# Dealing the turns of a two-layer decoder kernel anew: gate slices unit by unit, x loaded in smaller first parts from ScalarE's queue, narrower warm-up products

## Reference

```python
proj = h @ w_in                       # NSA: 1024 x 3632; HGRN2: 1024 x 4096
# layer 0 (NSA): q | k,v compressed | k,v selected | k,v window | gates | z
p_c = masked_softmax(q @ k_cmp, m_c)  # compressed branch; also picks the selected blocks
p_s = masked_softmax(q @ k_sel, m_s)
p_w = masked_softmax(q @ k_win, m_w)
o = g0 * (p_c @ v_cmp) + g1 * (p_s @ v_sel) + g2 * (p_w @ v_win)
x = x + (o * silu(z)) @ w_out
# layer 1 (HGRN2), per head: f, k = 1 - f, q, v from proj
state = exp(b_last) * state + (k * exp(b_last - b)).T @ v
o = (q * exp(b)) @ state + causal(q k^T * decay) @ v
x = x + (rmsnorm(o) * g_norm * silu(z)) @ w_out
out = rms_norm(x, final_norm)
```

## Time and profile before

| | us |
|---|---|
| median of 3 runs (318.56 to 318.68) | 318.58 |
| profiled execution | 319.03 |
| its span, first to last instruction | 316.8 |
| TensorE busy in the span | 307.6 |
| VectorE busy | 240.4 |
| ScalarE busy | 183.8 |

### The profile page before, as it was taken

One profiled execution on the slowest core, in us unless ns is written; L12 is line 12 of the kernel. 1 busy time (PEld: TensorE's weight loads), 2 busy tenths in 40 slices (PEclk: granted clock), 3 DMA queues, 4 the chain that ended last, 5 costly groups with the idle time before them and its releaser, 6 DMA issues.

```text
span 316.8 us, 5853 instructions
## 1 busy us (share of the span) xinstructions
PE 307.6 (97%) x2228; PEld 262.8 (83%) x2228; DVE 240.4 (76%) x423; ACT 183.8 (58%) x387; POOL 47.0 (15%) x51
## 2 busy tenths in 40 slices
PE   7999999999999999999999999999999989999993
PEld 5899788878899788877788889999997768888882
DVE  3969987899799878988748824477878997498941
ACT  4885262467794775866545744775264307897432
POOL 1003003031412341656000100000000100222000
PEclk9999999999999999999999999999999999999998
DMA  7999894756604800160270984374915233002011
GB/s 226 398 383 356 275 371 149 240 228 139 128 2 92 177 0 2 24 241 2 72 263 6 357 290 155 115 260 134 336 69 173 94 129 142 1 2 66 2 66 66
DMA packets 27819, 49.34 MB, mean 156 GB/s; under 512 B 2376, under 2 KB 6736, under 8 KB 27792
## 3 DMA queue, kind: packets, MB, share of 16 engines
q1 hardware_dynamic: 24896, 44.32, 43.0%
q10 hardware_dynamic: 2384, 2.63, 2.5%
q0 software_dynamic: 512, 2.03, 1.9%
HBM read 47.92 MB, written 1.05 MB: 155 GB/s over the span
## 4 chain that ended last, share of the span: by engine, by line
PE 78%; DVE 15%; issue 3%; DMA 2%; ACT 1%; SPq 0%; DVEq 0%; ACTq 0%
PE bank L589 73%; DVE w_lo L1105 3%; PE bank L768 2%; DVE nmax L1353 2%; DMA x_res<-in_x 2%; DVE qk L1164 1%; DVE prob_t L1365 1%; PE bank L633 1%; PE bank L691 1%; ACT prob L974 1%; DVE y_hg L1433 1%; DVE zT L1309 1%; PE bank L835 1%; DVE y_hg L1427 0%; DVE q L1280 0%
## 5 line engine op out<-in xcount | busy, mean ns | idle before, releaser
L1105 DVE TENSOR_TENSOR w_lo<-raw,w_hi 128x1024 fp32r<-128x1024 f32 (+1 forms) x80 | 86.8, 1138 | 19.3 <-ACT w_hi L865 19.3
L865 ACT ACTIVATE w_hi<-raw 128x1024 fp32r<-128x1024 f32 (+1 forms) x80 | 72.6, 966 | 15.7 <-PE bank L589 12.4
L589 PE MATMUL bank<-w_hi,h_hi 128*128 128x512 f32 x192 | 78.0, 406 | 0.0
L589 PE MATMUL bank<-w_hi,h_lo 128*128 128x512 f32 x192 | 75.1, 391 | 0.0
L589 PE MATMUL bank<-w_lo,h_hi 128*128 128x512 f32 x192 | 74.9, 390 | 0.0
L589 PE MATMUL bank<-h_hi,w_hi 128*128 128x256 f32 x224 | 64.7, 289 | 0.0
L589 PE MATMUL bank<-h_hi,w_lo 128*128 128x256 f32 x224 | 63.4, 283 | 0.0
L589 PE MATMUL bank<-h_lo,w_hi 128*128 128x256 f32 x224 | 63.4, 283 | 0.0
L589 PEld LDWEIGHTS bank<-h_lo,w_hi 128*128 128x128 f32 x224 | 42.9, 192 | 0.3
L589 PEld LDWEIGHTS bank<-h_hi,w_hi 128*128 128x128 f32 x224 | 43.0, 192 | 0.2
L589 PEld LDWEIGHTS bank<-h_hi,w_lo 128*128 128x128 f32 x224 | 42.9, 192 | 0.0
(11 more groups left out here) (207 smaller groups left out, 400.4 us busy)
## 6 DMA issues: line engine op xcount, KB each, us to landing
raw<-in_hg SPq DMA_DIRECT2D x16, 1024.0 KB, 7.0
raw<-in_nsa SPq DMA_DIRECT2D x10, 1024.0 KB, 7.6
raw<-in_nsa_out SPq DMA_DIRECT2D x8, 512.0 KB, 8.3
raw<-in_hg_out SPq DMA_DIRECT2D x4, 1024.0 KB, 6.2
raw<-in_nsa SPq DMA_DIRECT2D x2, 1120.0 KB, 7.4
raw<-in_nsa SPq DMA_DIRECT2D x8, 256.0 KB, 5.8
w<-in_w1k SPq DMA_DIRECT2D x2, 1024.0 KB, 12.8
w<-in_w1v ACTq DMA_DIRECT2D x2, 1024.0 KB, 6.8
```

Source lines behind the costliest of these rows:

```text
L589: return nc.tensor.matmul(o, lhsT, rhs, start=start, stop=stop, skip_group_check=True)
L865: m = nc.scalar.activation(dst, src, ACT.Copy)
L1105: m = V.tensor_tensor(lo, src, hi.bitcast(F32), ALU.subtract)
```

## The change

- `x` is loaded in three parts of each 128-row block (256, 256 and 512 columns). SyncE issues the first part of block 0 and the two wide parts; ScalarE issues the other three small ones before its table load. The bytes are the same.
- `HEAD` takes the first weight piece before the first pieces of `x`.
- The warm-up products are 2 of 256 columns, then 1 and 3 of 128, in place of 2, 1 and 2 of 256.
- `Z_ORDER` takes both token blocks of `V_Z0`, then both of `V_Z1`; before, the units alternated.
- `ORDER`, `H_ORDER`, `SPREAD`, `LAG`, `Z_LAG`, `CMP_LAG` and `PROD_LAG` have new values. The instructions and their shapes are otherwise the same.

```diff
-IDLE = (2, 1, 2)
+IDLE = ((S, 2), (P, 1), (P, 3))
-Z_LAG = 3
-Z_ORDER = [(V_Z0, 0), (V_Z1, 0), (V_Z0, 1), (V_Z1, 1)]
+Z_LAG = 2
+Z_ORDER = [(V_Z0, 0), (V_Z0, 1), (V_Z1, 0), (V_Z1, 1)]
-PROD_LAG = (5, 2)
+PROD_LAG = (4, 2)
-H_ORDER = 'aaaahhbbbbcccchhddeeeeddfFfFFFffFFFQFQQQQQQQGGGRGGGGGRRRRRRRzzllllzzllllzzllllzllllzllllzllllzzllllzoozxxzzzyyoommmyymnnnrrnrsrsss'
+H_ORDER = 'aaaahhbbbbcccchhddeeeeddfFfFFFffFFFQFQQQQQQQGGGGGRGGGRRRRRRzRzzllllzzzllllzzllllllllzllllzlllzzlzllllozoxxzzyyoommmyymnnnnsrrrrsss'
-FIRST_LOADS = [("x", 0, 0), ("w", 0), ("w", 1), ("x", 1, 0), ("w", 2), ("w", 3), ("x", 0, 1), ("x", 1, 1),
-               ("w", 4), ("w", 5), ("w", 6), ("w", 7)]
+X_PARTS = [slice(0, 2 * P), slice(2 * P, 4 * P), slice(4 * P, D)]
+FIRST_LOADS = (('x', 0, 0), ('w', 0), ('w', 1), ('w', 2), ('x', 0, 2), ('w', 3), ('x', 1, 2), ('w', 4), ('w', 5), ('w', 6), ('w', 7))
+ACT_LOADS = ((1, 0), (0, 1), (1, 1))
-CMP_LAG = 3
+CMP_LAG = 6
+        def load_x(eng, t, part):
+
+            cols = X_PARTS[part]
+            eng.dma_start(x[:, t, cols], t_in["x"][t * P:(t + 1) * P, cols]).then_inc(x_in[t][part], 16)
...
-                    for _ in range(IDLE[step[1]]):
-                        mm(bank[0][:, 0:S], rp[:, 0, 0:P], rp[:, 0, 0:S], True, True)
+                    wide, times = IDLE[step[1]]
+                    for _ in range(times):
+                        mm(bank[0][:, 0:wide], rp[:, 0, 0:P], rp[:, 0, 0:wide], True, True)
...
-                        pe.wait_ge(x_in[t][q // 2], 16)
+                        pe.wait_ge(x_in[t][min(q, 2)], 16)
...
+            for t, part in ACT_LOADS:
+                load_x(act, t, part)
```

More of the change, by code:

```diff
@@ L77 @@
 PROD_W = HD + HD // 2
-PROD_LAG = (5, 2)
+PROD_LAG = (4, 2)
 RECT_LV = (LAST_LV - 2, LAST_LV - 1)
-ORDER = 'HHAAHBHHBAAAHAHBBBABABCDCCrBCDDDgxEEFkGkEgFEFKIFIgIKKpIKgxLpkppgJkgqqgqsqszzszatgzztssbszztzszszzzctssvvvvtstsztzzavtsztvvvtststbsstvvvvtssostotsosctsvvvvttsvvttottvvvvtovvooo'
+ORDER = 'HHHAABHHHBAABAAHBABABBCDCCrCBDDDgxgEkEFGEEIKFFkFKIIKqIggKxppLkpkpgJgqqgszqsszzgatzzbsszzttzzszztcszsstvvvvstztzsavtsszztvvvtstsstsstbvvvvtssottosovvtcsvvtststvvtottvvvvtovvooo'
 HT_BANKS = ((4, 5, 6, 7), (0, 1, 4, 5))
-H_ORDER = 'aaaahhbbbbcccchhddeeeeddfFfFFFffFFFQFQQQQQQQGGGRGGGGGRRRRRRRzzllllzzllllzzllllzllllzllllzllllzzllllzoozxxzzzyyoommmyymnnnrrnrsrsss'
+H_ORDER = 'aaaahhbbbbcccchhddeeeeddfFfFFFffFFFQFQQQQQQQGGGGGRGGGRRRRRRzRzzllllzzzllllzzllllllllzllllzlllzzlzllllozoxxzzyyoommmyymnnnnsrrrrsss'
 CMP_BANKS = ((1, 1, 7), (7, 6, 1))
@@ L207, in split_places @@
     return places
-HEAD = [part for q in range(4) for t in range(TT)
-        for part in (("w", 2 * q + t), ("h", t, 2 * q), ("h", t, 2 * q + 1))]
-HEAD[0:4] = HEAD[1:3] + HEAD[0:1] + HEAD[3:4]
-FIRST_LOADS = [("x", 0, 0), ("w", 0), ("w", 1), ("x", 1, 0), ("w", 2), ("w", 3), ("x", 0, 1), ("x", 1, 1),
-               ("w", 4), ("w", 5), ("w", 6), ("w", 7)]
+HEAD = (('w', 0), ('h', 0, 0), ('h', 0, 1), ('w', 1), ('h', 1, 0), ('h', 1, 1), ('w', 2), ('h', 0, 2), ('h', 1, 2), ('h', 0, 3), ('h', 1, 3), ('w', 3), ('w', 4), ('h', 0, 4), ('h', 0, 5), ('w', 5), ('h', 0, 6), ('h', 0, 7), ('w', 6), ('w', 7), ('h', 1, 4), ('h', 1, 5), ('h', 1, 6), ('h', 1, 7))
+X_PARTS = [slice(0, 2 * P), slice(2 * P, 4 * P), slice(4 * P, D)]
+FIRST_LOADS = (('x', 0, 0), ('w', 0), ('w', 1), ('w', 2), ('x', 0, 2), ('w', 3), ('x', 1, 2), ('w', 4), ('w', 5), ('w', 6), ('w', 7))
+ACT_LOADS = ((1, 0), (0, 1), (1, 1))
 H_RANK = {part[1:]: n + 1 for n, part in enumerate(part for part in HEAD if part[0] == "h")}
@@ L222, in split_count @@
     return kk + 1 if u == 0 else KT + NQ * (u - 1) + kk // 2 + 1
-SPREAD = {U_KW: (0, 0, 3, 2), U_Q0: (7, 6, 29, 0), U_Q1: (0, 59, 13, 61), U_Z0: (0, 0, 4, 2), U_Z1: (3, 8, 5, 0), U_O0: (22, 18, 7, 37), U_O1: (44, 82, 83, 135), V_V0: (0, 2, 2, 2), V_V1: (0, 0, 26, 21), V_F0: (0, 0, 41, 5), V_Q0: (11, 3, 19, 73), V_F1: (0, 0, 6, 2), V_Q1: (3, 2, 26, 12), V_Z0: (1, 6, 2, 0), V_Z1: (2, 0, 14, 49), V_O0: (1, 3, 2, 5), V_O1: (5, 0, 2, 3)}
+SPREAD = {U_KW: (0, 0, 28, 27), U_Q0: (0, 20, 60, 2), U_Q1: (15, 41, 21, 43), U_Z0: (0, 3, 0, 0), U_Z1: (1, 8, 0, 9), U_O0: (11, 0, 8, 39), U_O1: (43, 103, 105, 152), V_V0: (0, 2, 0, 1), V_V1: (2, 0, 32, 42), V_F0: (0, 0, 23, 0), V_Q0: (11, 11, 12, 99), V_F1: (2, 3, 1, 2), V_Q1: (3, 2, 25, 9), V_Z0: (2, 3, 11, 22), V_Z1: (7, 0, 3, 55), V_O0: (9, 9, 0, 6), V_O1: (4, 0, 0, 1)}
 GATED_LAG = 6
-CMP_LAG = 3
+CMP_LAG = 6
 GATED_AT = [max(LAST[("pv", job)], LAST[Z_GROUPS[-1]] + job) for job in range(4)]
-LAG = {U_O0: 1, U_O1: 5, V_Z0: 4, U_Z0: 1, U_Q1: 10, V_O1: 2, V_Q0: 8, V_F1: 3, V_Z1: 4, V_F0: 8, V_V1: 2, U_Z1: 4, U_KW: 2, U_Q0: 2, V_V0: 1, V_O0: 2, V_Q1: 4}
+LAG = {U_O0: 11, U_O1: 6, V_Z0: 13, U_Z0: 3, U_Q1: 14, V_O1: 1, V_Q0: 1, V_F1: 4, V_Z1: 2, V_F0: 1, V_V1: 1, U_Z1: 3, U_KW: 2, U_Q0: 5, V_V0: 3, V_O0: 4, V_Q1: 1}
 SPLIT_HI_AT, SPLIT_LO_AT = split_places()
@@ L343, in program @@
         w1_in = [sem(f"w1_in{kv}") for kv in range(2)]
-        x_in = [[sem(f"x{t}_in{half}") for half in range(2)] for t in range(TT)]
+        x_in = [[sem(f"x{t}_in{part}") for part in range(len(X_PARTS))] for t in range(TT)]
         const_in = sem("const_in")
@@ L565, in _ @@
                         if what[0] == "x":
-                            _, t, part = what
-                            half = slice(part * UW, (part + 1) * UW)
-                            sp.dma_start(x[:, t, half], t_in["x"][t * P:(t + 1) * P, half]).then_inc(x_in[t][part], 16)
+                            load_x(sp, *what[1:])
                         else:
```

## The result

The changed kernel takes 321.25 us in the median of five runs (320.22 to 323.13; a sixth, disturbed one took 777.61, is left out of all comparisons, and would make the median 321.51) against 318.61 before: slower, ratio 1.008 with an interval of 1.0062 to 1.0098. 316.2 had been forecast, with a range up to 317.9. The profiled execution takes 321.78, its span is 319.7.

What follows compares the result with a forecast made beforehand. TensorE's queue of products was taken as the bound, busy 307.6 of 316.8 us. Head -0.2, changes of kind -1.0, attention -0.6 and levels -0.6 gave -2.4: 316.6 profiled, 316.2 for the median, range 315.3 to 317.9.

Steps and rivals of the forecast that it cites:

- rival (d): Head: the shorter warm-up lets TensorE's 1.2 GHz level last beyond 7.28; 317.6 (chance 0.04) or 319.6 (0.08).
- the slow end: Head: products run at half speed from 7.3 to about 14.5; +3.4, 319.6 us, chance 0.08.
- the milder case of (d): Head: the first three slices run at half speed, 0.6 hidden in the wait for x; +1.4, 317.6, chance 0.04.
- Head: Start of the kernel: transposes that waited for x until 9.9 come earlier; -0.2, between -0.5 and +0.1.
- 1,024 KB, again 7.24: Head: small x parts and two weight pieces total 1,024 KB, so they land at 7.24 as before.
- Fewer changes of kind: TensorE's order: 100 switch groups between fp32r products and other work in place of 112, ten at 0.1; -1.0.
- Rival (a): TensorE's order: switches cost nothing that can be had back; -1.4 in all, 317.2, chance 0.12.
- Attention: Attention: the prob_t copy comes 1.0 earlier on VectorE, so TensorE's waits of 0.52 and 0.2 shrink; -0.6.
- what is late next is the copy behind it, by 0.1 or 0.2: Attention: once the 0.52 wait is gone, the following copy is late by only 0.1 or 0.2.
- rival (b): Attention and levels: waits only move along VectorE's queue; -1.2, 317.4, chance 0.13.
- Levels: Recurrence levels: TensorE's two waits for decays shrink from 1.34 to about 0.7; -0.6, ends -1.3 and +0.3.

Runs made afterwards that it cites:

- e1: The changed kernel with the old loads, HEAD, warm-up products and first 19 letters of ORDER: 319.40 us, ratio 1.0026 to the kernel before.
- e5: The kernel before with the new head, but warm-up products all 256 columns wide as before: 319.32 us, ratio 1.0018.
- e2: The kernel before with the new head alone (two-queue loads, HEAD, narrow warm-up products, first 19 letters of ORDER): 320.94 us, ratio 1.0074.
- e7: The kernel before with the new head and narrow warm-up products, but all parts of x issued by SyncE: 319.18 us, ratio 1.0018.
- e11: The kernel before with the new head, all x parts issued by SyncE and warm-up products 256 wide: 319.01 us, ratio 1.0013.
- e10: The kernel before with two levels of the recurrence each cut in two by a gate slice (H_ORDER): 319.10 us, ratio 1.0015.
- e4: The kernel before with the new tables of layer 0 alone, without the new head: 319.88 us, ratio 1.0036.
- e3: The kernel before with the new tables of layer 1 alone (H_ORDER, Z_ORDER, PROD_LAG, V_ entries of SPREAD and LAG): 318.44 us, ratio 0.9991.
- e6: The kernel before with only the new, shorter warm-up products (2 of 256, then 1 and 3 of 128 columns): 319.56 us, ratio 1.0026.
- e15: The kernel before with the new tables of layer 0 alone, but CMP_LAG 5 in place of 6: 321.00 us, ratio 1.0073.

## Why the prediction was wrong

**The sign** fell twice: with the head (+2.2) and with the tables of layer 0 (+1.1). Either would have been enough against the 0.3 that layer 1 gained; e1, with the old head, is at ratio 1.0026. The larger part of the head's loss is rival (d), the clock: with wide warm-up products it is 0.5 (e5), with the new ones 2.2 (e2). The mechanism was named, on the evidence of the earlier trace rows, and given 0.12 in all and 0.08 for the slow end. Two steps made it too small. It was priced as if only the level at the start could last longer; in fact a raised array also falls back (8.7 to 12.07 in the profile after). And I put the landing of the last small part at 7.24 and reckoned only with the shorter warm-up: the late `x` made the idle time 1.16 and 0.67 us. The price of the clock itself was about right for the milder case of (d), three slices at half speed for +1.4: the eight products from 8.72 to 12.07 take 3.35 us, where at 0.23 each they take 1.84, a loss of 1.5. The slow end of (d) reckoned with twice that stretch; that the change ended on its side is due to layer 0 and to the changes of kind, not to the clock.

**Head, -0.2 predicted, +2.2 measured (e2).** The step that failed first is "1,024 KB, again 7.24". I named the other order, in which the third weight piece stands ahead of the last small part, and gave it 7.9 and +0.1; it landed at 8.2. The loads ran slower as well: in the changed kernel 185 and 212 GB/s were moved in the third and fourth microsecond, against 283 and 330 before. With the same small parts on one queue it was 204 and 319 (e7): the slow fourth microsecond goes with the two queues; why the third is slow isn't shown. What the forecast said of the far side was right: earlier products would only wait for the wide part of block 1 (e7, e11). With a sound warm-up and one queue the head is worth +0.2, not -0.2.

**Fewer changes of kind, -1.0 predicted, about 0 by the times of turns (no run has it alone).** Rival (a) was right for the groups that the change removes. I read half of a row pair: the second product of a slice starts late, but the turns ahead of it end early by the same amount. The groups that cost something, 0.35 each, are those of level products (e10), and the change has seven of them, as before: it joins two levels and cuts another in two. The count was generous too: taking slices against everything else, the strings have 87 changes before and 81 now, not 112 and 100.

**Attention, -0.6 predicted, +1.1 measured in e4 and 1.2 in its timeline, for all tables of layer 0.** The two waits for `prob_t` went, as forecast. But "what is late next is the copy behind it, by 0.1 or 0.2" was wrong: 0.5 at the normalized scores of block 0, 0.2 for GpSimd's `prob`, and small delays at other turns. By the shortest turns of the same kind and neighbours, the excess of TensorE's turns in layer 0 is 1.0 before and 2.1 in e4, of which the list of waits shows 0.7 in each. This goes the way of rival (b), but (b) had the gain come to nothing, and here it turned into a loss. Which entry of the tables makes it stays open: no single one that I tried brings it back, and the old places of the splits don't fit the new order.

**Levels, -0.6 predicted, -0.3 measured (e3).** The mechanism was right and its place too: two waits, at the second of the two levels that follow each other. They are 0.56 and 0.41, as in this timeline of the changed kernel:

```profile
262.70 1.12 PE L591 MATMUL bank<-qk 128*64 128x32 f32 x32 [0.56 <-DVE qk L1169]
264.23 1.13 PE L591 MATMUL bank<-qk 128*64 128x32 f32 x32 [0.41 <-DVE qk L1169]
```

The term was mis-sized: I had 0.4 to 0.7 for both, they sum to 0.97, and 1.34 - 0.97 is 0.4, where 0.3 was measured. The three slices in a row stand one level further up than the text on the change says; two slices stand ahead of the first of the two joined levels.

## What to carry to other kernels

Don't shorten the warm-up without looking at a dozen executions: the median of three can hide an upper heap. What the traces ask of warm-up products is that the array is up when the first real products begin, whatever their width; idle time of up to 1.02 us behind them did no harm once it had risen, and longer waits for the operand are a risk to the clock and not only a wait. A comparison of two single traces of a head is worth 0.5 us at most, since the same head started `U_KC` at 18.64 to 19.19. Price a change of order by whole groups from start to start, neighbours included, not by the first product behind them. Where the engine that serves the bound one is busy 85% of a stage, count a removed wait as moved until the queue behind it has been walked.

## What the runs showed of the hardware

- The same kernel came out at 318.4 to 318.7 or at 320.3 to 321.0 by chance (e6), on the same chip; the profiled one, of the upper heap, had TensorE's array at 1.2 GHz for the first real products (0.43 apart).
- The same four records of warm-up products took 1.91, 1.52 or 1.06 us in executions of the same head (before, e15, e3): the array rose from 1.2 to 2.4 GHz behind them or at different points within them. It stayed up over 1.02 us of idle time (e3), and fell behind 1.16 and 0.67 us of it (the change).
- The granted clock of a window read 1.00 while products ran at half speed throughout (e2), and over the first rise from that level (e6); it read 0.57 where the clock fell and rose within the record (the change).
- One more group of level products between fp32r slices costs 0.35 us (e10), one more of transposes or scores nothing measurable (the turns' times).
- Of the Trainium skill, page "DMA: Bandwidth & Descriptors", section "Issuing engines are not separate DMA queues", which says that this saves only the time to issue, the runs agree that nothing is won: the part issued by ScalarE at 2.25 landed at 8.2, and the one issued by SyncE at 3.06, in another order of the weight pieces, landed at 7.0.
